# Attention scores from high and low parts: three one-pass products per head in place of one plain product

## What is computed

```python
def dilated_attn_mixer(h, positions, w_qkv, w_o):
    qkv = (h @ w_qkv).reshape(Bz, S, 3, N_HEADS, HEAD_DIM)
    q = partial_rotary(qkv[:, :, 0], positions)
    k = partial_rotary(qkv[:, :, 1], positions)
    v = qkv[:, :, 2]
    o = dilated_attention(q, k, v).astype(h.dtype)
    return o.reshape(Bz, S, ATTN_WIDTH) @ w_o
...
    s = jnp.einsum('bgnqhd,bgnkhd->bgnhqk', qblk, kb).astype(jnp.float32) * (hd ** -0.5)
    s = jnp.where(valid[:, None], s, NEG_INF)
    p = jnp.exp(s - m)
```

## Time and profile before

| | us |
|---|---|
| median of 3 runs (range) | 1480.32 (1479.22 to 1483.79) |
| profiled execution, its own time | 1479.5 |
| its span | 1477.7 |
| attention: first scores to last `weigh` | 863.6 to 968.5 |
| PE busy, share of the span | 1295.2, 88% |

### The profile page before, as it was taken

The page is one execution under the profiler, slowest core; times in us unless marked ns, Lnnn a source line. Parts: engine busy times, 40 slices in busy tenths (PEclk is TensorE's granted clock), DMA queues, the critical chain, the costliest instruction groups (busy, mean ns, idle before and its releaser), DMA issues.

```text
span 1477.7 us, 14182 instructions
## 1 busy us (share of the span) xinstructions
PE 1295.2 (88%) x4817; PEld 822.9 (56%) x4817; DVE 911.3 (62%) x1312; ACT 582.7 (39%) x790; POOL 168.8 (11%) x181
## 2 busy tenths in 40 slices
PE   2799999938999999984899999999289999999881
PEld 1445444525667777641788854445266666777430
DVE  5678962467777777713866377715667777777114
ACT  2246200226555555502422156613355555555001
POOL 4000001010000000002000047700110000000002
PEclk9999999958999999997899999999589999999996
DMA  8964676035999999893375440031359999998444
GB/s 277 377 223 129 236 242 270 29 138 185 375 374 365 361 365 381 312 341 125 129 272 171 143 171 1 1 128 51 132 206 368 383 372 365 371 367 311 153 177 185
DMA packets 79744, 353.13 MB, mean 239 GB/s; under 512 B 12825, under 2 KB 13009, under 8 KB 70737
## 3 DMA queue, kind: packets, MB, share of 16 engines
q1 hardware_dynamic: 64704, 326.65, 59.7%
q0 software_dynamic: 8352, 20.46, 3.8%
q10 hardware_dynamic: 6640, 5.42, 1.2%
HBM read 334.15 MB, written 28.31 MB: 245 GB/s over the span
## 4 chain that ended last, share of the span: by engine, by line
PE 84%; DVE 7%; ACT 2%; issue 2%; DMA 2%; ACTq 1%; POOL 1%; DVEq 0%; POOLq 0%; SPq 0%
PE ps L1576 24%; PE ps L1587 16%; PE ps L1489 10%; PE ps L1675 9%; PE ps L1517 8%; PE ps L1567 3%; PE ps L1562 2%; PE ps L1719 2%; PE ps L1747 2%; PE ps L1733 2%; PE ps L1463 2%; PE ps L1581 1%; PE ps L1530 1%; PE ps L1499 1%; ACTq L654 1%
## 5 line engine op out<-in xcount | busy, mean ns | idle before, releaser
L1587 PE MATMUL ps<-slab_ring,scratch 128*128 128x512 f32 x560 | 246.5, 593 | 3.4 <-ACT scratch L801 2.1
L1576 PE MATMUL ps<-slab_ring_r,gate_rows_r 128*128 128x512 f32 x512 | 202.2, 395 | 0.0
L1587 PEld LDWEIGHTS ps<-slab_ring,scratch 128*128 128x128 f32 x560 | 105.8, 190 | 124.2 <-issue 117.3
L1258 DVE TENSOR_TENSOR slab_ring_r<-slab_ring,h_t_r 128x2048 fp32r<-128x2048 f32 x64 | 143.8, 2288 | 22.6 <-ACT h_t_r L753 22.5
L1489 PE MATMUL ps<-h_t,slab_ring 128*128 128x512 f32 x320 | 146.3, 618 | 0.0
L1675 PE MATMUL ps<-slab_ring_r 128*128 128x512 f32 x384 | 122.7, 401 | 2.9 <-DVE h_t_r L931 2.9
L1576 PE MATMUL ps<-h_t_r,gate_rows_r 128*128 128x512 f32 x256 | 106.3, 415 | 14.7 <-DVE scratch_r L1252 11.1
L753 ACT ACTIVATE h_t_r<-slab_ring 128x2048 fp32r<-128x2048 f32 x64 | 118.4, 1901 | 0.2 <-issue 0.2
L1576 PEld LDWEIGHTS ps<-slab_ring_r,gate_rows_r 128*128 128x128 f32 x512 | 98.3, 192 | 19.3 <-issue 0.5
L1489 PEld LDWEIGHTS ps<-h_t,slab_ring 128*128 128x128 f32 x320 | 63.2, 199 | 79.2 <-issue 79.1
L1576 PE MATMUL ps<-h_t_r,scratch_r 128*128 128x512 f32 x256 | 102.6, 401 | 0.0
(11 more groups left out here) (286 smaller groups left out, 2010.7 us busy)
## 6 DMA issues: line engine op xcount, KB each, us to landing
slab_ring<-in_expert_w_gate_dram SPq DMA_DIRECT2D x35, 2048.0 KB, 9.6
slab_ring<-in_expert_w_up_dram SPq DMA_DIRECT2D x35, 2048.0 KB, 9.6
slab_ring<-in_expert_w_down_dram SPq DMA_DIRECT2D x35, 2048.0 KB, 9.3
mod_ring<-in_mod_w_dram SPq DMA_DIRECT2D x64, 512.0 KB, 4.6
y_rows<-scratch SPq DMA_DIRECT2D x35, 512.0 KB, 10.2
slab_ring<-in_mod_w_dram SPq DMA_DIRECT2D x32, 512.0 KB, 4.7
slab_ring<-in_w_qkv_dram SPq DMA_DIRECT2D x6, 2048.0 KB, 11.5
slab_ring<-in_w_in_ab_dram SPq DMA_DIRECT2D x5, 2048.0 KB, 19.1
```

The source lines that it names most:

```text
L1258: tt_(rest, w, top.bitcast(F32), ALU.subtract).then_inc(low_ready[c], 1)
L1576: ins = pe.matmul(ps[:, bank, :], x, w, start=(kt == 0 and i == 0), stop=(kt == KT - 1 and i == 2))
L1587: ins = pe.matmul(ps[:, 5 + h, :], hidT[:, f, :], w[:, 2 * f + h, :], start=(f == 0), stop=(f == FT - 1))
```

## The change

`take_qk` now makes two tiles of each turned tile. ACT writes a rounded copy (the high part, type fp32r) and DVE then subtracts it from the PSUM bank and writes the rest (the low part, fp32r too). Each score product becomes three: high by high, high by low and low by high, in the two row halves in turn, accumulated in the same bank. The low parts live in slots 1 and 2 of `slab_ring`, so the first two expert loads of layer 1 wait until all 64 scores are done (`s_ready`, 64).

```diff
-    def qk_tile(j):
-        return (KTR, QT)[j // 8][:, j % 8, :]
+    QK_LOW_SLOT = (1, 2)
+    def qk_high(j):
+        return (HT_r, R_r[:, 8:16, :])[j // 8][:, j % 8, :]
+    def qk_low(j):
+        return ring_r[:, QK_LOW_SLOT[j // 8], j % 8, :]
...
-                    1: [(qkv_ready, 24), (qkv_ready, 24), (av_ready, 8), (av_ready, 8), (y_ready, 16), (y_ready, 16)]}[l]
+                    1: [(s_ready, 2 * UNITS), (s_ready, 2 * UNITS), (av_ready, 8), (av_ready, 8), (y_ready, 16), (y_ready, 16)]}[l]
...
             act.wait_ge(qk_turned, j + 1)
-            act.activation(qk_tile(j), ps[:, QK_BANK[j], :], ACT.Copy).then_inc(qk_act, 1)
-        for j in range(0, 10, 2):
+            act.activation(qk_high(j), ps[:, QK_BANK[j], :], ACT.Copy).then_inc(qk_act, 1)
+        for j in range(9):
             take_qk(j)
...
-            if i < 3:
-                take_qk(10 + 2 * i)
+            if i < 4:
+                for j in range(9 + 2 * i, min(11 + 2 * i, 16)):
+                    take_qk(j)
...
             v.wait_ge(qk_turned, j + 1)
-            v.tensor_copy(qk_tile(j), ps[:, QK_BANK[j], :]).then_inc(qk_dve, 1)
-        take_qk(1)
-        take_qk(3)
-        take_qk(5)
+            v.wait_ge(qk_act, j + 1)
+            tt_(qk_low(j), ps[:, QK_BANK[j], :], qk_high(j).bitcast(F32), ALU.subtract).then_inc(qk_dve, 1)
+        for j in range(6):
+            take_qk(j)
         mod_take(LAYERS * PARTS - 1)
-        take_qk(7)
+        for j in range(6, 9):
+            take_qk(j)
...
             if i < 4:
-                take_qk(9 + 2 * i)
+                for j in range(9 + 2 * i, min(11 + 2 * i, 16)):
+                    take_qk(j)
...
-            pe.wait_ge((qk_act, qk_dve)[j % 2], j // 2 + 1)
+            pe.wait_ge(qk_dve, j + 1)
...
-            for par in range(2):
-                r0 = HD * par
-                pe.matmul(ps[:, 2 * (u % 2) + par, :], QT[r0:r0 + HD, hp, it * P:(it + 1) * P], KTR[r0:r0 + HD, hp, :], start=True, stop=True).then_inc(s_ready, 1)
+            q_high, q_low, k_high, k_low = qk_high(8 + hp), qk_low(8 + hp), qk_high(hp), qk_low(hp)
+            for i, (q, k) in enumerate(((q_high, k_high), (q_high, k_low), (q_low, k_high))):
+                for par in range(2):
+                    rows_ = slice(HD * par, HD * par + HD)
+                    ins = pe.matmul(ps[:, 2 * (u % 2) + par, :], q[rows_, it * P:(it + 1) * P], k[rows_, :], start=(i == 0), stop=(i == 2))
+                    if i == 2:
+                        ins.then_inc(s_ready, 1)
```

## The result

The changed kernel takes 1485.91 us (median of 20 runs, 1481.68 to 1490.53) against 1479.53 for the kernel before in its own 20 runs: ratio 1.0038, interval 1.003 to 1.0045. That is slower by 6.4 us in the medians and by 5.6 in the ratio; forecast were 5.6 us and 1486. The profiled execution took 1487.89 us, 2 us above the median, with a span of 1486.1.

A forecast was written before the change was run, and what follows sets the result against it. PE was taken to bound most stages. Terms +1.5, +8.2 and -4.1 sum to +5.6 on the profiled 1479.5, giving 1485.1; the median, 0.8 higher, gives 1485.9, say 1486 us, with 8 in 10 from 1481 to 1491.

The forecast's parts named there:

- The product: PE's score block in units 8 to 31: 0.89 us instead of 1.06, gaining 0.17 a unit, -4.1 us over 24 units.
- Ahead of the loop: Before the first scores: DVE's added subtractions make the first score step come at 866.35 instead of 864.86, +1.5 us.
- Iterations 0 to 3: Start of the attention loop: DVE's subtractions wait for ACT's takes behind its exponentials; 17.25 us against 9.05, +8.2 us.
- term for iteration 2: Iteration 2 of the loop's start: adds DVE's scaling of 0.5 besides a reciprocal, given as 4.65 us.
- Units 4 to 8: Unit 4 to unit 7: POOL sets the pace as before, so no term; the backlog isn't made good.
- The loads: Expert 0's gate and up weights, issued near 960 instead of 857.40: they cost nothing if landing within 20 us.
- the rival with a chance of 0.2: Slow start of the loop: the granted clock falls and PE's work slows, together +3.2 us, giving 1489; chance 0.2.
- A granted clock under 1 between 865 and 900: Start of the attention loop: PE's clock below full in this stretch, listed as a sign of the prediction being wrong.
- Full overlap of the halves: PE's score products: both row halves work at once, three pairs each as long as one 0.227 us product.
- the other rivals: Score block: halves don't overlap, 1503, chance 0.07; pairs pay weight loads, 1491, 0.07; weight load and switch vanish, 1480, 0.06.

The follow-up runs named there:

- act_first: The changed kernel with ACT's takes put ahead of its two exponentials in iterations 0 to 3; 1479.86 us, ratio 1.0001 to the kernel before.
- no_act_wait: The changed kernel with DVE's subtraction reading the residual stream in SBUF, so nothing of ACT's is waited for; 1476.99 us, ratio 0.9978 to the kernel before.
- sub_later: The changed kernel with each of the last seven subtractions one iteration behind ACT's take; 1479.31 us, ratio 0.9994 to the kernel before.
- late_loads: The kernel before with only the gate and up loads of layer 1's expert 0 waiting for the last scores; 1480.18 us against 1480.20, ratio 0.9995.
- half_by_half: The changed kernel issuing all three score products of one row half, then all three of the other; 1485.87 us, ratio 1.0041 to the kernel before.
- busy_units: The changed kernel with six repeated one-pass pairs ahead of the score products of units 0 to 3; 1486.81 us, ratio 1.0036 to the kernel before.
- busy_ramp: The changed kernel with two plain products ahead of the first scores and six repeated pairs in units 0 to 3; 1487.16 us, ratio 1.0049 to the kernel before.

## Why the prediction was right

**The product, -4.1 forecast, -3.5 measured (units 8 to 31).** The block was costed at 0.10 + 0.11 + 3 x 0.227 = 0.89, and is 0.89. A unit averages 67.73 / 23 = 2.94 us where it took 71.24 / 23 = 3.10: a gain of 3.51 / 23 = 0.15 and not 0.17. The forecast counted 24 units, the stage has 23 steps, which is 0.17 of the missing 0.6. In some units the block is 0.91; what delays them the trace doesn't show.

**Ahead of the loop, +1.5 forecast, +2.0 measured.** The subtractions ran at the pitch assumed: six in 3.68 us, and the last ended 866.51 - 858.25 = 8.26 us after the first transpose, where the forecast had 865.15 - 856.79 = 8.36. The missing 0.5 is PE's: the first scores ran at a lowered clock, and DVE's first score step came 868.38 - 866.61 = 1.77 us behind them and not 1.05. In `act_first`, at full clock, it came 1.08 behind, and the lead is 9.44 - 8.08 = 1.4 longer than before.

**Iterations 0 to 3, +8.2 forecast, +8.5 measured.** Starts of units' score steps are 4.04, 4.1, 4.6 and 4.8 apart; forecast were 4.1, 4.25, 4.65 and 4.25. The subtraction started 2.84 behind the score step, forecast 2.8. The last iteration is longer by the clock, 0.7: at full clock it takes 4.11, and the four together 16.87 where 17.25 was forecast. So the close agreement is in part luck, the clock's cost making up for working that was 0.4 too long. (Its term for iteration 2 also writes 4.65 where 4.25 + 0.5 is 4.75; 4.61 was measured.) `no_act_wait`, `act_first` and `sub_later` show that the wait behind ACT's exponentials is the mechanism, worth about 6 us; the rest is the added operations, 1.65 at most, and the clock.

**Units 4 to 8, nothing forecast, -0.3 measured.** They took 9.96 us and 10.27 before; the backlog was not made good there, as argued.

**The loads, 0 forecast.** Shown by `late_loads`; the changed kernel's gate loads land 10.8 us after their issue (median of two), and the first use is 92 us behind it.

**The sum.** The four stages differ from the forecast by +0.5, +0.3, -0.3 and +0.6, so +6.75 where +5.6 stood. About 1.4 of the 6.75 is the clock's, in this one execution; without it the stages would give about +5.4. The medians differ by 6.4, the ratio gives 5.6.

**The rivals.** The clock did fall, as the rival with a chance of 0.2 said. A granted clock under 1 between 865 and 900 also stood among the prediction's own signs of being wrong. In the profiled execution it cost 0.7 at the first scores and 0.7 in iteration 3, and not 3.2: DVE and ACT set the pace of the start, and PE was at 0.96 of full from 883 to 887, before the units in which it counts. That it was back by then was luck: in `half_by_half` it wasn't, and units 4 to 8 paid 1.9, by the rival's mechanism. The forecast ought to have carried such a term. How often the changed kernel's other runs pay it isn't shown; they spread from 1481.68 to 1490.53. The Trainium skill, TensorE: Matmul & The Clock Gate, Part 3, would have a weight load overlap matmuls in flight only in other rows; the load at 912.62 behind a pair that began at 912.51, with pairs 0.23 apart, contradicts it for one-pass products also. Full overlap of the halves held, and the switch ahead of and behind the block stayed, so none of the other rivals came true.

## What to carry to other kernels

A second engine's operation that reads what a first engine has just made inherits everything queued ahead of it on the first: cost it by the position in both queues, not by its own 0.6 us. In a short start phase such a chain between two lightly loaded engines can outweigh a gain on the engine that bounds the long phase behind it. When a change helps in the steady part and loses at the start, split it by experiment and look at the order of the queues before giving the idea up. And read the granted clock beside every stage that is compared: here it made 0.7 to 1.9 us where differences of 2 to 9 were compared.

## What the runs showed of the hardware that wasn't expected

- Matmuls of two row halves ran side by side even when all three of one half stood ahead of the other's in the queue: 0.90 for the block in that order, 0.89 with the halves in turn.
- PE's clock was lowered in the start though PE's busy time was between 1.81 and 4.00 in 4 us; after the same idle time of 2.55 us it was full in `act_first` and `half_by_half` (1.00 from 863 to 867) and lowered in `busy_units` (0.78 from 862 to 866, 1.00 from 870 on). With the added matmuls of `busy_ramp` it was full from 863 to 883 and lowered from 883 to 891. What exactly decides it is left open.
